# Attention scores computed with keys on the partitions, their maxima taken from a first rough product

## The reference

```python
s = jnp.einsum('bqhd,bkhd->bhqk', qn, k_nope) + jnp.einsum('bqhd,bkd->bhqk', qr, k_rope)
pr = jax.nn.softmax(s.astype(jnp.float32) * scale, axis=-1).astype(v.dtype)
return jnp.einsum('bhqk,bkhd->bqhd', pr, v)
...
x = x + jnp.concatenate([attn, pool], axis=-1) @ w_out
```

## Time and profile before

| | |
|---|---|
| median of three runs | 1146.49 us |
| the profiled execution's own time | 1144.88 us |
| its span | 1143.1 us |
| PE busy | 1117.8 us (98%) |
| DVE busy | 826.1 us (72%) |
| ACT busy | 555.4 us (49%) |
| POOL busy | 464.2 us (41%) |

### The profile page before, as it was taken

How to read it: one execution, slowest core, us unless ns; L and a number is a source line. 1 busy time by engine, 2 the same in 40 slices (tenths; PEclk the granted TensorE clock), 3 DMA queues, 4 the chain that set the end, 5 groups by cost and what they waited for, 6 DMA issues and landing times.

```text
span 1143.1 us, 15837 instructions
## 1 busy us (share of the span) xinstructions
PE 1117.8 (98%) x5146; PEld 896.6 (78%) x5146; DVE 826.1 (72%) x1170; ACT 555.4 (49%) x986; POOL 464.2 (41%) x405
## 2 busy tenths in 40 slices
PE   8999999999999989999999999999999999999996
PEld 7787766665888867888888888888888888888885
DVE  7784976674468899878787878787876757757555
ACT  6312687775223454545454545454554545533332
POOL 0185642322566046765676567655310202211000
PEclk9999999999999999999999999999999999999999
DMA  6610000104652126444544454445896565533341
GB/s 209 222 44 26 1 12 13 38 19 164 204 202 104 56 81 205 165 138 152 178 165 138 154 176 165 138 155 172 330 344 204 190 197 192 168 108 118 92 143 74
DMA packets 138431, 161.60 MB, mean 141 GB/s; under 512 B 8755, under 2 KB 105354, under 8 KB 133770
## 3 DMA queue, kind: packets, MB, share of 16 engines
q1 hardware_dynamic: 138080, 160.82, 42.0%
q10 hardware_dynamic: 298, 0.11, 0.0%
HBM read 115.55 MB, written 45.35 MB: 141 GB/s over the span
## 4 chain that ended last, share of the span: by engine, by line
PE 86%; DVE 10%; issue 2%; ACT 1%; POOL 1%; DMA 0%; DVEq 0%; SPq 0%; POOLq 0%; ACTq 0%
PE ps L298 26%; PE ps L299 26%; PE ps L300 26%; PE ps L869 2%; PE ps L850 2%; DVE WL L2050 1%; PE ps L711 1%; PE ps L861 1%; DVE XL L1727 1%; DVE SF L2149 1%; DVE SF L2157 1%; DVE WDHL L1907 1%; DVE col L1918 1%; DVE XT L1721 0%; DVE R L1900 0%
## 5 line engine op out<-in xcount | busy, mean ns | idle before, releaser
L298 PE MATMUL ps<-XH,WH 128*128 128x512 f32 x722 | 287.1, 398 | 0.8 <-DVE WL L339 0.5
L300 PE MATMUL ps<-XH,WL 128*128 128x512 f32 x722 | 281.2, 390 | 0.0
L299 PE MATMUL ps<-XL,WH 128*128 128x512 f32 x722 | 281.1, 389 | 0.0
L298 PEld LDWEIGHTS ps<-XH,WH 128*128 128x128 f32 x722 | 135.6, 188 | 32.4 <-issue 3.0
L299 PEld LDWEIGHTS ps<-XL,WH 128*128 128x128 f32 x722 | 135.7, 188 | 29.1 <-issue 2.2
L300 PEld LDWEIGHTS ps<-XH,WL 128*128 128x128 f32 x722 | 135.5, 188 | 28.5
L298 PE MATMUL ps<-GHL,WH 128*128 128x512 f32 x394 | 153.6, 390 | 0.8 <-DVE WL L2050 0.7
L300 PE MATMUL ps<-GHL,WL 128*128 128x512 f32 x394 | 153.3, 389 | 0.0
L299 PE MATMUL ps<-GHL,WH 128*128 128x512 f32 x394 | 153.3, 389 | 0.0
L334 ACT ACTIVATE WH<-WR 128x1024 fp32r<-128x1024 f32 (+3 forms) x45 | 45.5, 1011 | 138.7 <-PE ps L300 129.4
L1476 ACT ACTIVATE SF<-ps,col 128x512 f32<-128x512 f32 x88 | 68.2, 778 | 74.6 <-PE ps L300 65.6
(11 more groups left out here) (241 smaller groups left out, 2250.8 us busy)
## 6 DMA issues: line engine op xcount, KB each, us to landing
TL<-in_w_up SPq DMA_DIRECT2D x48, 256.0 KB, 3.6
s_scratch<-XT SPq DMA_DIRECT2D x11, 1024.0 KB, 4.7
XT<-in_w_down SPq DMA_DIRECT2D x11, 1024.0 KB, 6.5
t_scratch<-XT SPq DMA_DIRECT2D x11, 1024.0 KB, 3.8
WR<-t_scratch SPq DMA_DIRECT2D x44, 256.0 KB, 2.7
TL<-s_scratch SPq DMA_DIRECT2D x44, 256.0 KB, 2.9
WR<-in_w_up SPq DMA_DIRECT2D x40, 256.0 KB, 3.5
WR<-in_w_down SPq DMA_DIRECT2D x33, 256.0 KB, 3.7
```

The costliest lines, as they stand in the source:

```text
L298: pe.matmul(out, wh, xh, start=first, stop=False, skip_group_check=skip)
L299: pe.matmul(out, wh, xl, start=False, stop=False, skip_group_check=skip)
L300: return pe.matmul(out, wl, xh, start=False, stop=last, skip_group_check=skip)
```

## The change

The scores are computed with the keys on the partitions from the start, so that nothing has to be transposed. A step's work is now:

- PE: `rough`, one product of high halves (128 queries x 512 keys), three steps ahead, from which DVE takes the row maximum (into `MXR`, fp32r).
- PE: after four of them `turn_max`, a product with the identity (4 x 128), whose result ACT copies in four pieces into four extra rows of the high queries (`max_rows`); the high keys have ones in those rows. So the product itself subtracts the maximum.
- PE: `scores`, three products with keys as the stationary operand, two steps behind; ACT's `exponent` writes straight into `PT`.
- POOL: `key_sum` adds the four key tiles of each head (three additions, 48 in all); PE's `total` multiplies them by ones, DVE transposes them in blocks of 32 x 32, inverts 16 columns, ACT spreads them, DVE transposes them back and multiplies.
- POOL takes over 11 of the 16 `q_low` and loses `row_diagonals`.
- The first `project_k` and `project_q` move into the last input tile, the first six eighths of the first output tile (`OUT_EARLY`) move into the last pair. DVE's `pooled(7, 1, 3)` and `latent_low` move behind the first rotation. POOL fills the rows of ones before its first `root`.

The diff, cut to its core:

```diff
-        PB = [SF[:, 0:512], SF[:, 512:1024], SF[:, 4608:5120]]
+        SUM = [SF[:, 2560:3072], diag[:, :, :].rearrange("p t q -> p (t q)"), SF[:, 0:512], SF[:, 512:1024]]
+        RT = SF[:, 4608:5120]
...
+                            pe.wait_ge(c_lo, 2)
+                            pe.wait_ge(kr_done, 4)
+                            project_k(0, 0, mix_hi, 6)
+                            pe.wait_ge(c_lo, 4)
+                            project_q(0, 0, acc_free, 14)
...
+            def rough(v):
+                n, t = divmod(v, TT)
+                s, h = divmod(n % 4, 2)
                 if t == 0:
-                    pe.wait_ge(q_lo, i * 4 + j + 1)
-                    pe.wait_ge(k_lo, i * 4 + j + 1)
-                if i * 16 + u >= 3:
-                    pe.wait_ge(exp_done, i * 16 + u - 2)
-                tok = slice(t * P, (t + 1) * P)
-                ins = mm3(pe, s_bank(i * 16 + u)[:, :], QH[0:HEAD, s, h, tok], QL[0:HEAD, s, h, tok],
-                          KH[0:HEAD, s, h, :], KL[0:HEAD, s, h, :], True, True)
-                ins.then_inc(s_ready, 1)
-            def turn(i, u):
-                pe.wait_ge(exp_done, i * 16 + u + 1)
-                if i == 0 and u < 2:
-                    pe.wait_ge(v_copied, u + 1)
+                    pe.wait_ge(q_hi, n + 1)
+                    pe.wait_ge(k_hi, n + 1)
+                if v >= 2:
+                    pe.wait_ge(max_ready, v - 1)
+                pe.matmul(m_bank(v)[:, :], QH[0:HEAD, s, h, t * P:(t + 1) * P], KH[0:HEAD, s, h, :],
+                          start=True, stop=True).then_inc(m_ready, 1)
+            def turn_max(n):
+                pe.wait_ge(max_ready, 4 * n + 4)
+                if n:
+                    pe.wait_ge(max_row, n)
                 else:
-                    pe.wait_ge(pt_ready, i * 16 + u - 1)
-                for k in range(TT):
-                    ins = pe.transpose(ps[4 + u % 2][:, k * P:(k + 1) * P], p_buf(i * 16 + u)[:, k * P:(k + 1) * P], ident[:, :])
-                ins.then_inc(p_tr, 1)
+                    pe.wait_ge(acc_free, 14)
+                    pe.wait_ge(consts_set, 4)
+                pe.matmul(ps[1][0:TT, 0:P], MXR[:, n % 2, 0:TT], ident_r[:, :], start=True, stop=True).then_inc(max_turned, 1)
+            def scores(v):
+                n, k = divmod(v, TT)
+                s, h = divmod(n % 4, 2)
+                if k == 0:
+                    pe.wait_ge(max_row, n + 1)
+                    pe.wait_ge(q_lo, n + 1)
+                    pe.wait_ge(k_lo, n + 1)
+                if v < 2:
+                    pe.wait_ge(v_copied, v + 1)
+                else:
+                    pe.wait_ge(exp_done, v - 1)
+                keys = slice(k * P, (k + 1) * P)
+                o = s_bank(v)[:, :]
+                pe.matmul(o, KH[0:MAXED, s, h, keys], QH[0:MAXED, s, h, :], start=True, stop=False)
+                pe.matmul(o, KH[0:HEAD, s, h, keys], QL[0:HEAD, s, h, :], start=False, stop=False)
+                pe.matmul(o, KL[0:HEAD, s, h, keys], QH[0:HEAD, s, h, :], start=False, stop=True).then_inc(s_ready, 1)
...
+            def total(i, s):
+                pe.wait_ge(sum_step, 3 * (i * 4 + 2 * s + 2))
+                if i or s:
+                    pe.wait_ge(rr_copied, i * 2 + s)
+                pe.wait_ge(v_copied, i * 2 + s + 1 + (i < HEADS // 2 - 1) * (2 - s))
+                for h in range(2):
+                    ins = pe.matmul(ps[7][h * V_DIM:(h + 1) * V_DIM, :], ones[:, 0:V_DIM], SUM[2 * s + h], start=True, stop=True)
+                ins.then_inc(rr_ready, 1)
+            OUT_ORDER = [4, 5, 6, 7, 0, 1, 2, 3]
+            OUT_EARLY = [7, 8, 10, 12, 14, 15]
+            def out_piece(s, m, k, first, last):
+                n = T_OUT + s * KT + m
+                return mm3(pe, ps[m % 4][:, :], WH[:, slot(n), k, :], WL[:, slot(n), k, :],
+                           XH[:, s, k, :], XL[:, s, k, :], first, last)
...
+                    v = 4 * TT * i + u
+                    if v == 1:
+                        turn_max(0)
+                    if v + 3 < 2 * HEADS * TT:
+                        rough(v + 3)
+                    if v >= 2:
+                        scores(v - 2)
+                    if u % TT == 1 and v > 1:
+                        turn_max(v // TT)
...
+                    if u == 13:
+                        total(i, 0)
...
+            def exponent(v):
+                n, k = divmod(v, TT)
+                act.wait_ge(s_ready, v + 1)
+                if v in (8, 12):
+                    act.wait_ge(d_lo, 7 if v == 8 else 8)
+                    act.wait_ge(keep_lo, 3 if v == 8 else 6)
+                if k == 0 and n >= 4:
+                    act.wait_ge(o_ready, n // 2 - 1)
+                    act.wait_ge(sum_step, 3 * (n - 3))
+                act.activation(PT[:, (n + 2) % 4, k, :], s_bank(v)[:, :], ACT.Exp).then_inc(exp_done, 1)
+            def max_rows(n):
+                s, h = divmod(n % 4, 2)
+                act.wait_ge(max_turned, n + 1)
+                if n >= 4:
+                    act.wait_ge(s_ready, 4 * (n - 3))
+                for a in range(TT):
+                    ins = act.activation(QH[HEAD:MAXED, s, h, a * P:(a + 1) * P], ps[1][0:TT, 0:P], ACT.Copy,
+                                         scale=ident[0:TT, a:a + 1])
+                ins.then_inc(max_row, 1)
+            def spread_rc(i, s):
+                act.wait_ge(rc_ready, 2 * (i * 2 + s) + 1)
+                act.activation(RT.rearrange("p (b c) -> p b c", c=32), col[:, RC:RC + 16].unsqueeze(2).broadcast_to([P, 16, 32]),
+                               ACT.Copy).then_inc(o_hi, 1)
...
-            def maximum(i, u):
-                dve.wait_ge(s_ready, i * 16 + u + 1)
-                dve.tensor_reduce(col[:, NB + u % 4:NB + u % 4 + 1], s_bank(i * 16 + u)[:, :], AX_X, ALU.max,
-                                  negate=True).then_inc(max_ready, 1)
+            def maximum(v):
+                n, k = divmod(v, TT)
+                dve.wait_ge(m_ready, v + 1)
+                dve.tensor_reduce(MXR[:, n % 2, k:k + 1], m_bank(v)[:, :], AX_X, ALU.max, negate=True).then_inc(max_ready, 1)
             def inverse(i, s):
-                dve.wait_ge(exp_done, i * 16 + 8 * (s + 1))
-                if i:
-                    dve.wait_ge(dr_ready, i * 2 + s - 1)
-                dve.reciprocal(col[:, RC + 8 * s:RC + 8 * s + 8], col[:, RS + 8 * s:RS + 8 * s + 8]).then_inc(rc_ready, 1)
+                n = i * 2 + s
+                dve.wait_ge(rr_ready, n + 1)
+                dve.transpose(RT, ps[7][:, :]).then_inc(rr_copied, 1)
+                dve.wait_ge(rr_copied, n + 1)
+                dve.reciprocal(col[:, RC:RC + 16].unsqueeze(2), RT.rearrange("p (b c) -> p b c", c=32)[:, :, 0:1]).then_inc(rc_ready, 1)
             def scale_rows(i, s):
-                dve.wait_ge(o_ready, i * 2 + s + 1)
-                dve.wait_ge(rr_copied, i * 2 + s + 1)
+                n = i * 2 + s
+                dve.wait_ge(o_hi, 2 * n + 1)
+                dve.transpose(RB[:, :], RT).then_inc(rc_ready, 1)
+                dve.wait_ge(o_ready, n + 1)
+                dve.wait_ge(rc_ready, 2 * n + 2)
                 dve.tensor_tensor(RB[:, :], ps[6][:, :], RB[:, :], ALU.mult).then_inc(o_norm, 1)
...
+            pool.tensor_scalar(ident_r[:, :], ident[:, :], 1.0, 1.0, ALU.mult, ALU.mult).then_inc(consts_set, 1)
+            pool.wait_ge(consts_set, 3)
+            pool.tensor_scalar(KH[HEAD:MAXED].rearrange("p s h t -> p (s h t)"), ones[HEAD:MAXED, 0:1].broadcast_to([TT, 2 * NSEQ * S]),
+                               1.0, 1.0, ALU.mult, ALU.mult).then_inc(consts_set, 1)
+            pool.wait_ge(consts_set, 4)
             pool.wait_ge(consts_set, 2)
...
+            def key_sum(n, k):
+                a, buf = PT[:, (n + 2) % 4], SUM[n % 4]
+                pool.wait_ge(exp_done, 4 * n + k + 1)
+                if k == 1:
+                    if n >= 4:
+                        pool.wait_ge(rr_ready, n // 2 - 1)
+                    pool.tensor_tensor(buf, a[:, 0, :], a[:, 1, :], ALU.add).then_inc(sum_step, 1)
+                else:
+                    pool.wait_ge(sum_step, 3 * n + k - 1)
+                    pool.tensor_tensor(buf, buf, a[:, k, :], ALU.add).then_inc(sum_step, 1)
...
```

471 lines of the change are left out of this document (233 added, 238 removed).

## The result

| | median | runs | ratio to the kernel before, 95% interval |
|---|---|---|---|
| kernel before | 1147.83 us | 7 | |
| changed kernel | 1154.89 us | 7 | 1.0062 [1.0049, 1.0076] |

The changed kernel is 7.1 us slower. Forecast were 1142.3 us and a range up to 1151; both were wrong, and so was the sign. The profiled execution took 1154.41 us (span 1152.6). From the first row of the changed stretch to the start of the second output tile it needs 175.4 us (118.43 to 293.87), where the kernel before needs 167.0 and the forecast had 161.8. I call this the stage; behind it the two kernels differ by 0.3 us in these two profiles.

The account below looks back on a forecast made before the run. PE, busy 98% of the span, bounds the kernel: 1144.88 profiled - 9.9 (list) - 10.1 (old waits) + 15.8 (new waits) = 1140.7, so a median of 1142.3 us; 8-in-10 range 1134.5 to 1151.

Parts of the forecast that it names:

- the sign: Whole kernel: the changed kernel would be faster, its median 4.2 us less than before; chance of faster 0.48.
- The granted clock is 1.00 in all of them ... so neither is in question.: Stretches of the changed stage, about 117.7 to 284.7 us: full clock throughout, DMA share at most 0.34, neither in question.
- The list: PE's instructions in the stage: turns of 28.5 us go, 18.6 us of new work comes, 9.9 us less.
- the waits before: PE's waits in the old stage: 166.96 us less 156.8 of listed work, 10.1 us, all going with the old order.
- First pair, waits: PE's waits in attention's first pair, DVE setting the pace: 10.0 us, between 7 and 15.
- The wait on POOL: First pair, at `total(0, 0)`: PE waits 4.5 us for POOL's sixth addition, 11.0 us of chain against 6.5.
- The entry's four waits: First pair: 1.9 us at `project_q(0, 2)`, 1.7 at the fifth `rough`, 1.9 together at the next two head ends.
- Later pairs and the last: Chain ends uncovered behind `total`: 1.2 us a pair, 2.4 for two; last pair 2.4 (1 to 5).
- The start: Before the first input tile: POOL's fill of ones slows DVE's first weight split, 1.0 us, between 0 and 1.5.
- Covered waits: Rival, whole stage: the order hides more, about 9 us of waits stay, 1136 us; chance 0.22.
- Slow row copies: Rival, head ends: row copies take 0.42 us instead of 0.28, adding 4.5 us, 1147 us; chance 0.10.
- The lock: Rival, mostly first pair: POOL and two-input DVE instructions block each other, adding 9 us, 1151 us; chance 0.20.

Follow-up runs that it names:

- run 2: Changed kernel plus 89 unread identity transposes on PE filling three first-pair waits, which stay: 1150.03 us, ratio 1.0024 to the kernel before.
- run 14: Kernel before plus one artificial PE wait in the second pair, for 18 small unread POOL additions: 1155.62 us, ratio 1.0064.
- run 9: Changed kernel with `total` and the second `weigh` exchanged in pairs behind the first, so `weigh` stands behind `turn_max`: 1152.13 us, ratio 1.0041.
- run 13: Changed kernel with first pair reordered, `weigh` behind maxima in all pairs, POOL's ones fill moved, 27 transposes in PE's waits: 1146.16 us, ratio 0.9993.
- run 1: Changed kernel with POOL's six first-pair key additions placed between the low halves instead of behind the last: 1153.10 us, ratio 1.0050.
- The mended order: Changed kernel with first pair reordered, chain ends covered by `weigh` or query projection, ones fill moved, no filling transposes: 1143.89 us, ratio 0.9963.

## Why the prediction was wrong

- **The step that failed first: "The granted clock is 1.00 in all of them ... so neither is in question."** I took the clock of the kernel before for a property of the stage. It was a property of its order, in which PE has no wait of over 0.9 us in this stage. The forecast itself put 10 us of waits on PE into the first pair, and priced each at its length alone. Measured: 6.1 us of slow products in the profile; 4.9 us in the medians when only the clock was held up (run 2); 2.1 us beyond a wait of 6.1 in the profile of run 14. The clock doesn't explain the sign by itself: with it held up the kernel still takes 1150.0 us, 7.7 over the forecast and above the kernel before. The rest are the list and the waits.
- **The list, and the waits before.** As a rest, the list fell by 5.6 us instead of 9.9. About 2 us of this gap are the forecast's 10.1 us of waits before, which were about 8: it priced 348 products at 0.229, where this stage starts them up to 0.235 apart, and took what was left for waits (it announces three rows for them and names two). The other 2 us are the new list itself. A step without a turn starts its products 0.235 apart, as the score rows already showed, and takes 0.94, not 0.92; without waits a pair takes 35.7 us, not 35.1. More of it I can't assign.
- **First pair, waits.** 10.0 forecast, 11.6 measured. The wait on POOL was named with its cause, at 4.5 us; it is 5.37. The entry's four waits were forecast with 5.5 us in sum, and the two large ones are 1.61 and 1.85.
- **Later pairs and the last.** 1.2 a pair forecast, 1.6 and 1.9 measured; 2.4 and 2.9 for the last. They stand where forecast, behind each `total` and none behind `weigh` (run 9 takes the first away). The parts: a row copy 0.275 us (0.28 forecast), `STREAM_TRANSPOSE` 0.72 (0.69).

```profile
132.49 1.10 ACT L1361 ACTIVATE GHL<-ps,ident 4x128 fp32r<-4x128 f32 x4 [5.61 <-PE ps L860]
```

```profile
171.53 0.72 DVE L1979 STREAM_TRANSPOSE SF<-ps 128x512 f32<-128x512 f32 x1 [6.04 <-PE ps L901]
```

- **The start.** 0.7 us late (1.0 forecast). The lock is real (split 2.00 us), but with the split back at 1.21 in run 13 PE started only 0.16 us sooner: most of the 0.7 isn't the lock's.
- **The rivals.** Covered waits: refuted. Slow row copies: refuted. The lock: its price of 1151 was the nearest to the result, but not as its cause; in the changed kernel it lengthened one split to 1.68 us, with a wait of PE of 0.32 us behind it, and it reached PE only when the additions were moved onto the splits (run 1).

With what was measured, 1142.3 + 6.1 (clock) + 3.2 (waits) + 4.3 (list and waits before) - 0.3 (start) = 1155.6 us, against 1154.9. The list's term is a rest, so this sum shows the sizes and proves nothing by closing. The mended order reaches 1143.9, near the forecast: the new scheme can give that much, its first pair and its chain ends took it away. It doesn't bear the forecast's sum out, since it is another order, with other waits.

## What to carry to other kernels

Where a change puts a wait of PE into a stretch that had none, price the wait and the half-speed products behind it, and read the granted clock of such a stretch as an outcome, not as a given. Here waits of 0.7 us close together brought a fall, as one of 5 us did, and one of 2.2 us did not; so the length of a wait alone doesn't tell. A chain at a hand-over is better covered by moving long work behind its start than by starting it sooner, and a fall of the clock costs little or nothing where another engine sets the pace.

## What the runs showed of the hardware that was not expected

The clock also falls at places that no edit touched, and not in every profile: at 55 to 58 us in the profiles of twelve of the 17 kernels made from the changed one and in run 14, though not in the changed kernel's own; at 370 to 398 us in eight of the 17; and at 412 to 438 us in nine, and in the kernel before. Most last 3.4 us.

What such a fall costs depends on the place. At 370 to 398 us it is 1.6 us: the same 250 products take 57.3 us in the eight profiles that have it and 55.7 in the others. At 412 to 438 us it is nothing: 64.3 us for 250 products with it and without. There PE waits for DVE in either case. The kernel before, and then PE's row at the same place in both kernels:

```profile
412.00:416.00 4.00, 1.87 (x6) 0.83 0.09 26
416.00:420.00 4.00, 4.00 (x15) 0.74 0.13 39
```

```profile
414.38 0.58 PE L298 MATMUL ps<-CHL,WH 128*128 128x512 f32 x1 [2.13 <-DVE WL L2050]
```

```profile
423.57 0.50 PE L299 MATMUL ps<-CHL,WH 128*128 128x512 f32 x1 [2.13 <-DVE WL L2106]
```

The same wait of 2.13 us on the same split stands in both profiles. The clock fell with it in the kernel before (at 414.66) and stayed at 1.00 in the changed one. So a wait can bring the clock down (runs 2 and 14), but one of this length doesn't do so each time, and what decides it no run here shows.

A second scatter isn't the clock's: the same 250 products, at about 800 to 880 us, take between 56.7 and 59.2 us with the clock at 1.00, by a few short waits. Both are why medians don't follow the stages closely.
